# Spreading the reciprocals of the softmax sums: GpSimd-issued transfers through a scratch tensor in place of a TensorE transpose

## The reference

```
# layer 0: neighbourhood attention with a context (latent tokens), and
s = einsum(q, k) * scale + bias            # keys of a window, and all 256 context tokens
p = softmax(concat([s_lat, s_ctx]))
o = p_lat @ v_blk + p_ctx @ vc
# dense_attn: the same without a window, for the 256 context tokens
# layer 1: sliding window of three blocks of 128 keys, a context, and a sink
p = softmax(concat([s_lat, s_ctx, s_sink]))[without the sink]
o = p_lat @ v_w + p_ctx @ vc
y = merge(o) * silu(gate)
```

## Time and profile before

| | us |
|---|---|
| median of 3 runs | 1530.75 (1529.42 to 1531.55) |
| the profiled execution | 1529.01 |
| its span | 1527.2 |
| PE busy in it | 1481.0 (97%) |
| DVE busy | 774.3 (51%) |
| ACT busy | 572.4 (37%) |
| POOL busy | 96.3 (6%) |

### The profile page before, as it was taken

How to read it: one execution, slowest core, us unless ns; L and a number is a source line. 1 busy time by engine, 2 the same in 40 slices (tenths; PEclk the granted TensorE clock), 3 DMA queues, 4 the chain that set the end, 5 groups by cost and what they waited for, 6 DMA issues and landing times.

```text
span 1527.2 us, 24584 instructions
## 1 busy us (share of the span) xinstructions
PE 1481.0 (97%) x9608; PEld 1024.3 (67%) x9608; DVE 774.3 (51%) x1670; ACT 572.4 (37%) x1323; POOL 96.3 (6%) x152
## 2 busy tenths in 40 slices
PE   7999999999999999999999999999999999998996
PEld 4575786577567577665588866678655455557985
DVE  3134565422222321432577855345668466776776
ACT  0134365533332422443202443122343763664034
POOL 0000000000000000000000000300031221111000
PEclk9999999999999999999999999999999999999998
DMA  9300020240421421501234621222121200101553
GB/s 378 118 28 15 15 108 23 86 164 28 175 87 64 155 73 63 210 15 39 100 126 155 211 79 50 81 60 73 49 69 53 111 24 5 42 28 50 156 172 121
DMA packets 72032, 139.74 MB, mean 91 GB/s; under 512 B 6656, under 2 KB 44588, under 8 KB 70572
## 3 DMA queue, kind: packets, MB, share of 16 engines
q1 hardware_dynamic: 66604, 135.55, 25.9%
q10 hardware_dynamic: 5312, 2.62, 0.6%
HBM read 125.43 MB, written 12.71 MB: 90 GB/s over the span
## 4 chain that ended last, share of the span: by engine, by line
PE 88%; DVE 6%; DMA 2%; ACT 2%; issue 1%; SPq 0%; DVEq 0%; ACTq 0%
PE mixed L1521 14%; PE proj L1521 12%; PE mixed L1471 5%; PE proj L1508 5%; PE turned L1666 5%; PE mixed L1505 5%; PE mixed L1576 5%; PE turned L1648 4%; PE proj L1576 4%; PE scores L1471 4%; PE proj L1505 3%; PE scores L1626 3%; PE scores L1629 2%; PE proj L1471 1%; PE scores L1521 1%; PE scores L1799 1%
## 5 line engine op out<-in xcount | busy, mean ns | idle before, releaser
L1521 PE MATMUL mixed<-hT,weights 128*128 128x512 f32 (+1 forms) x560 | 207.6, 519 | 0.2
L1521 PE MATMUL proj<-hT,weights 128*128 128x512 f32 (+1 forms) x480 | 187.2, 538 | 2.0 <-DMA weights<-in_weights 1.7
L1521 PEld LDWEIGHTS mixed<-hT,weights 128*128 128x128 f32 x560 | 103.4, 191 | 79.2 <-issue 73.1
L1521 PEld LDWEIGHTS proj<-hT,weights 128*128 128x128 f32 x480 | 88.1, 190 | 77.1 <-issue 70.8
L2488 ACT ACTIVATE work<-turned 128x512 f32<-128x512 f32 (+2 forms) x136 | 72.7, 535 | 144.8 <-PE turned L1648 108.9
L2184 DVE TENSOR_TENSOR yT<-turned,work 128x128 f32<-128x128 f32 x72 | 21.0, 292 | 158.1 <-PE turned L1666 154.6
L2488 ACT ACTIVATE work<-work,stat 128x640 f32<-128x640 f32 (+8 forms) x98 | 74.0, 755 | 30.7 <-DVE stat L2155 28.5
L1508 PE MATMUL proj<-weights,hT 128*128 128x128 f32 x672 | 77.8, 275 | 0.2 <-ACT kvV L2488 0.2
L1508 PEld LDWEIGHTS proj<-weights,hT 128*128 128x128 f32 x672 | 76.4, 192 | 0.5 <-ACT kvV L2488 0.4
L1648 PEld LDWEIGHTS turned<-consts,work 128*128 128x128 f32 (+3 forms) x448 | 49.1, 139 | 36.4 <-issue 22.1
L1505 PE MATMUL mixed<-weights,hT 128*128 128x256 f32 x320 | 72.0, 380 | 0.0
(11 more groups left out here) (394 smaller groups left out, 2778.8 us busy)
## 6 DMA issues: line engine op xcount, KB each, us to landing
weights<-in_weights SPq DMA_DIRECT2D x130, 512.0 KB, 4.2
tables<-in_bias SPq DMA_DIRECT2D x8, 1281.0 KB, 6.9
pair<-in_weights SPq DMA_DIRECT2D x20, 512.0 KB, 6.5
hT<-in_xT SPq DMA_DIRECT2D x8, 640.0 KB, 16.0
yT<-in_weights SPq DMA_DIRECT2D x8, 512.0 KB, 9.0
work<-in_xT SPq DMA_DIRECT2D x16, 256.0 KB, 2.7
x1T<-yT SPq DMA_DIRECT2D x8, 512.0 KB, 4.0
work<-rows SPq DMA_DIRECT2D x32, 128.0 KB, 3.3
```

The costliest lines, as they stand in the source:

```text
L1521: last = nc.tensor.matmul(PJ[BANK_OF[u]][:, 0:n], weights[:, w % WBUFS, k, :], src[:, k, t0:t0 + n], start=(k == 0), stop=(k == KT - 1))
```

## The change

`turn_groups` no longer adds an item for the sums. PE's transpose L1644 and POOL's copy L2795 go, and with them the buffers `sums_wide`. In their place:

- In its step `recip` of unit k, POOL issues two transfers, one to a head: a column of `stat` (128 partitions, 4 bytes each) to a row of a scratch tensor in DRAM, `sums`. Their landing is `sums_kept` of k.
- In its step `pv` of unit k, POOL waits for `sums_kept` of k+1 and for `att_out` of k-1, and then issues two transfers for unit k+1: the row of each head back from DRAM into 64 partitions of `prob_t`, 512 bytes each. Their landing is `sums_loaded` of k+1. Only then, in layer 1, does it wait for `sums_loaded` of k and multiply by the gate (`sums_gated` of k).
- DVE's L2184 waits for `sums_loaded` in layer 0, and for `sums_gated` in layer 1 as before.

The groups shrink: where five chunks made 4, 4 and 3 items they make 4, 4 and 2. The 8 context units go from two groups to one, the 8 units of four chunks in layer 1 from three to two. The table `MOVED` goes from 109 entries to 125: 4 that named `ptrans` steps are dropped and 20 are added, of which two are

```diff
+    (('recip', ('att', 1, 3, 6)), -8),
+    (('recip', ('att', 1, 2, 6)), -2),
```

The rest of the diff, without the table and the lists of names:

```diff
 def turn_groups(unit):
 
-    items = [(h, o, w) for h in range(2) for o, w, _ in unit.chunks] + [None]
+    items = [(h, o, w) for h in range(2) for o, w, _ in unit.chunks]
     return [items[x:x + 4] for x in range(0, len(items), 4)]
...
                 for x, item in enumerate(group):
                     to = TP[g % 2][:, x * P:(x + 1) * P]
-                    if item is None:
-                        pe.wait_ge(*at(("sums_wide", uid)))
-                        last = nc.tensor.transpose(to, sums_wide[uid[3] % 2], ident)
-                        continue
...
-                if number(uid) + 1 < 4 * N_UNITS[l]:
+                if number(uid) + 1 < 4 * N_UNITS[l] and len(turn_groups(unit_of(before(uid, -1)))) > 1:
                     pe.wait_ge(*at(("pt", before(uid, -1), 1)))
...
+                if before(uid, 4):
+                    dve.wait_ge(*at(("sums_kept", before(uid, 4))))
                 link(V.reciprocal(st[:, 6:8], st[:, 2:4]), ("recip", uid))
...
                 dve.wait_ge(*at(("pv", uid)))
-                if l:
-                    dve.wait_ge(*at(("sums_gated", uid)))
+                dve.wait_ge(*at(("sums_gated" if l else "sums_loaded", uid)))
...
         def _(engine):
             pool = Queue(engine)
 
-            def s_ptrans(uid, unit, g):
-
-                if uid[1] and g == len(turn_groups(unit)) - 1:
-                    _, l, j, i = uid
+            def s_recip(uid, unit):
+
+                pool.wait_ge(*at(("recip", uid)))
+                for h in range(2):
+                    nc.gpsimd.dma_start(a["sums"][uid[1], number(uid), h, :].unsqueeze(1),
+                                        stat[:, number(uid) % 4, 6 + h:7 + h]).then_inc(
+                        *up(f"sums_kept{number(uid) % 2}", *([("sums_kept", uid)] if h else []), by=16))
+
+            def spread_sums(uid):
+
+                at_col = 2 * len(unit_of(uid).chunks) * P
+                pool.wait_ge(*at(("sums_kept", uid)))
+                if before(uid, 2):
+                    pool.wait_ge(*at(("att_out", before(uid, 2))))
+                for h in range(2):
+                    nc.gpsimd.dma_start(prob_t[uid[3] % 2][h * DH:(h + 1) * DH, at_col:at_col + P],
+                                        a["sums"][uid[1], number(uid), h:h + 1, :].broadcast_to([DH, P])).then_inc(
+                        *up(f"sums_loaded{number(uid) % 2}", *([("sums_loaded", uid)] if h else []), by=16))
+
+            def s_pv(uid, unit):
+
+                _, l, j, i = uid
+                if number(uid) == 0:
+                    spread_sums(uid)
+                if number(uid) + 1 < 4 * N_UNITS[l]:
+                    spread_sums(before(uid, -1))
+                if l:
                     t0 = max(x[0] for x in CHUNKS_LAT if x[0] <= unit.t * P)
-                    pool.wait_ge(*at(("pt", uid, g)))
+                    pool.wait_ge(*at(("sums_loaded", uid)))
                     pool.wait_ge(*at(("gate_early", 4 + j, t0)))
                     at_col = 2 * len(unit.chunks) * P
                     sums = prob_t[i % 2][:, at_col:at_col + P]
                     nc.gpsimd.tensor_tensor(sums, sums, unit_tokens(yT[:, 4 + j, :], unit), ALU.mult).then_inc(
                         *up("pool_done", ("sums_gated", uid)))
-
-            def s_recip(uid, unit):
-                pool.wait_ge(*at(("recip", uid)))
-                if before(uid, 2):
-                    two_back = before(uid, 2)
-                    pool.wait_ge(*at(("turned", two_back, len(turn_groups(unit_of(two_back))) - 1)))
-                sums = stat[:, number(uid) % 4, 6:8].unsqueeze(2).broadcast_to([P, 2, DH])
-                nc.gpsimd.tensor_copy(sums_wide[uid[3] % 2].rearrange("p (h n) -> p h n", h=2), sums).then_inc(
-                    *up("pool_done", ("sums_wide", uid)))
```

30 lines of the change are left out of this document (22 added, 8 removed).

## The result

| | median, us | lowest to highest |
|---|---|---|
| before (4 runs, one of them beside the changed kernel) | 1530.09 | 1526.37 to 1531.55 |
| after (4 runs) | 1708.24 | 1703.50 to 1712.32 |

A forecast was written before the change was run, and what follows sets the result against it. PE's work was taken as the bound. Removed -11.7, added +3 in layer 1, moved steps 0: -8.7 from 1529.0 gives 1520.3; the median lies 1.7 higher, so 1522.0 us (own range 1516 to 1527, with rivals 1514 to 1545).

The forecast's parts named there:

- Its own sign of being wrong: Layer 1: L2184 waiting for POOL's gate in most units, the stretch from 1202 us exceeding 202 us, PE idling there.
- What it removes, -11.7: PE's 72 transposes 7.9 us, idle time ahead of them 2.8, ACT's shorter copies 1; between -7.9 and -19.5.
- POOL's issue, 0.6: Each transfer issue on POOL takes 0.6 us, chosen between SP's rows of 0.33 and 0.78.
- rival 1: Layer 1, 1202 to 1404: POOL's issue is dear and the ring paces the layer; 1541 to 1560 us, chance 0.23.
- the ring: Layer 1: reciprocal of k+1, transfers, gate and L2184 of k, reciprocal of k+2 wait in a circle; +3 us.
- rival 2: End of layer 1: busy DVE holds up POOL, stretching issues to 1.17 us; 1539 us, chance 0.12.
- The landing: Layer 1 sum: each new transfer lands 1.9 us after its issue, as the smallest transfer in the rows did.
- the same formula: Layer 1, reciprocal of k+1 to L2184 of k: start 0.23, issue, landing, two issues, gate 0.46; 4.4, rounded to 4.5 us.
- mean room of 6.2: Layer 1, old trace: mean time from reciprocal of k+1 to L2184 of k over 31 pairs; smallest 3.43 us.
- the dear end, 5.1: Highest landing assumed, 5.1 us after issue begins; in layer 1 it made the need 8.5 us, lack some 75 us.
- So layer 0 keeps its whole gain.: Layer 0: the way takes at most 12.0 us, inside the tightest room of 13.92 us, so no loss.
- The moved steps, 0 plus or minus 3: Twenty new MOVED entries shift steps by one to ten places, only winning or losing PE idle time; 0 ± 3 us.

The follow-up runs named there:

- no_transfers: The changed kernel with its four transfers a unit replaced by one POOL copy into prob_t, factors not turned (output wrong): 1520.53 us, ratio 0.9942.
- stores_beside: The kernel before, transposes kept, with the 144 POOL stores of 4-byte pieces added beside it, read by nobody: 1622.13 us, ratio 1.0604.
- layer1_only: The changed kernel with the change in layer 1 alone, layer 0 keeping its transposes, moved steps kept: 1677.21 us, ratio 1.0952.

## Why the prediction was wrong

It forecast 1522.0 with a range to 1545, and measured were 1708. Its own sign of being wrong did show: L2184 (L2196 now) waits for POOL's gate in 29 of 32 units of layer 1.

- **What it removes, -11.7.** About right: no_transfers gave -10.2, and PE's busy time fell by 12.0 us there. Without the added moves it was -5.6, a little less than the cheap end of 7.9.
- **POOL's issue, 0.6.** Right: 552 ns in the median and 709 at most over all 144 stores, 530 and 549 for the spreads. Rivals 1 and 2 both needed a dear or a stretched issue. Neither was there, with the second issue 0.56 us behind the first. What rival 1 said of the place and the mechanism came true, that the ring paces layer 1, but by the landing and not by the issue. The rule of the Trainium skill (SBUF — State Buffer, section SBUF: two separate sides) that rival 2 cited has no visible effect on the issues, 709 ns at most; whether DVE was ever in a two-port mode beside one of them no run shows, so the rule is neither borne out nor refuted. The gate took 0.47.
- **The landing, "the landing of the smallest transfer, 1.9, since these carry 0.5 KB and 32 KB".** This is the step that failed. The row was that of a single load of 62 KB on SP. A landing was taken from the bytes, and the form, 128 writes of 4 bytes side by side, had no row. 7.4 us were measured. With it the same formula gives 0.48 + 0.56 + 7.4 + 1.15 + 0.47 + 0.13 to the start on DVE = 10.2 us. Against a mean room of 6.2 this is 4 us a unit, and 3.6 us were lost for each of the 32 units, (317.6 - 201.2) / 32. Taken over the 31 rooms one by one, as the prediction does, a need of 10.2 us lacks 126 us in sum, and layer 1 lost 116. The ring was right, and its size was off by its largest term. Even the dear end, 5.1, lay below: it was the dearer of two rows taken, though the same trace has landings of up to 16.0 (640 KB), and no row showed this form. The spreads' landing was taken as 1.9 too and has a median of 3.0, but next to nothing waits for it in layer 1.
- **"So layer 0 keeps its whole gain."** Wrong, and by another way than the one looked at. Only the way from reciprocal to multiplication was compared with the room of 13.92 us. What the stores do to the other transfers, which PE waits for in layer 0, was not asked at all: "the SP queue keeps its order of transfers" was taken to mean that it keeps its times. stores_beside shows 73 us in layer 0 and 92 in all for the greater part by this. The mark set for it (L2184 waits for a transfer in layer 0) did show, 7 times for 23.6 us, but it is the smaller part.
- **The moved steps, 0 plus or minus 3.** Without transfers the two runs allow it (between nothing and 7 us gained). It does not hold where the transposes are kept, where the table costs 10.6 us in all and 3.9 in layer 1.
- **The clock.** The sum had no term for it. PE's busy time in layer 1 grew by 37 us at a mean clock of 0.85. How much of this is in the 116 us can't be told, since the ring paces the layer while PE waits.

Open: what in the memory or the DMA engine makes neighbouring small writes slow, at which distance between 4 and 64 bytes it ends, and why the same stores cost 63 us in layer 0 of one kernel and 93 in another.

## What to carry to other kernels

Price a transfer by its form: for a form that no row shows, its landing has no upper bound from other rows, and one small run of it, timed beside the untouched kernel, is worth more than a sum. Don't write many small pieces side by side into DRAM (4 bytes apart they were dear, 64 bytes apart they were not); turn or widen them on an engine first, or space them. And ask of every new transfer not only who waits for it, but also whose transfers share its engines, and what stands behind its wait in the issuing queue.

## What the runs showed of the hardware

- A store of 128 pieces of 4 bytes: 1.8 us to landing with 64 or 512 bytes from piece to piece, 7.4 us (the second of two) with 4 bytes, and 7.6 in the median of 64 such stores in layer1_only. Pieces of 8 bytes side by side 3.5 us, of 128 bytes (8 pieces) 1.7 to 2.6 in three kernels, of 256 bytes (128 pieces) 1.8.
- Such neighbouring stores slow other queues: 24 issues of SP's from 20.73 to 38.15 us in stores_beside, the landing of weights from 4.2 to 5.1 us in the changed kernel, the tables from 6.9 to 10.8. The queue that issues them makes no difference (7.4 us from POOL, 7.7 from ACT).
- A POOL-issued transfer occupies POOL for 0.52 to 0.56 us in the median with 64 or 128 pieces, and for 0.62 to 0.63 in the store of 8 pieces; an ACT-issued one occupies ACT for 0.40 (0.325 to 2.869).
- A 32x32 block transpose of 128x64 on VectorE took 0.245 us.
